# One tile of tokens summed in PSUM by a one-hot product over all experts; gate products and gate loads ahead of up; two shared groups before the expert loop and four inside it

## The reference

```python
scores = sigmoid(xt @ w_router)                       # xt = h, 544 tokens; 128 experts
_, idx = top_k(scores + b_router, 8)
gate = sel / sum(sel) * 2.5                           # sel = scores of the eight picked
h = silu(xb @ w_e1[e]) * (xb @ w_e3[e])               # xb: the tokens of expert e; 1024 -> 256
yb = (h @ w_e2[e]) * w[:, None]                       # w: their gates; 256 -> 1024
routed = zeros.at[tok].add(yb)                        # over all experts
shared = (silu(xt @ w_s1) * (xt @ w_s3)) @ w_s2       # one shared expert of 256
y = layer_norm(ALPHA * h + shared + routed)
```

## Time and profile before

| | us |
|---|---|
| median of three runs | 1943.91 |
| the profiled execution | 1941.7 |
| its span (first to last instruction) | 1939.9 |
| expert loop, first product to last output product | 825.3 to 1887.5 |
| busy: PE, DVE, ACT, POOL | 1777.5, 603.8, 392.7, 366.2 |
| mean granted TensorE clock | 0.966 |

### The profile page before, as it was taken

The page is one execution under the profiler, slowest core; times in us unless marked ns, Lnnn a source line. Parts: engine busy times, 40 slices in busy tenths (PEclk is TensorE's granted clock), DMA queues, the critical chain, the costliest instruction groups (busy, mean ns, idle before and its releaser), DMA issues.

```text
span 1939.9 us, 29734 instructions
## 1 busy us (share of the span) xinstructions
PE 1777.5 (92%) x10770; PEld 1051.4 (54%) x10770; DVE 603.8 (31%) x1504; ACT 392.7 (20%) x928; POOL 366.2 (19%) x529
## 2 busy tenths in 40 slices
PE   7999999999999999997899999988888888888887
PEld 6857778888888874643444444433333333333332
DVE  1296756873234213521122112211111111111113
ACT  0114455551221002211111111111111111111112
...
GB/s 122 141 133 120 87 66 50 3 36 53 137 80 134 87 61 207 223 335 421 421 419 413 417 413 412 419 407 400 412 397 410 409 411 404 407 399 416 399 406 238
DMA packets 162463, 529.82 MB, mean 273 GB/s; under 512 B 22173, under 2 KB 89039, under 8 KB 111821
## 3 DMA queue, kind: packets, MB, share of 16 engines
...
## 4 chain that ended last, share of the span: by engine, by line
PE 55%; DMA 36%; DVE 3%; SPq 2%; issue 2%; ACT 1%; DVEq 1%; ACTq 0%; POOLq 0%
DMA arena<-in_w_e 35%; PE bank L2088 14%; PE bank L1460 9%; PE bank L522 5%; PE bank L1467 5%; PE bank L558 4%; PE bank L1218 4%; PE bank L1951 3%; SPq L1376 2%; PE bank L547 1%; PE bank L2011 1%; PE bank L2106 1%; PE bank L1977 1%; DVEq L1326 1%; DVE arena L932 1%
## 5 line engine op out<-in xcount | busy, mean ns | idle before, releaser
L2088 PE MATMUL bank<-arena 128*64 128x512 f32 x2048 | 505.1, 651 | 122.5 <-DMA arena<-in_w_e 121.2
L2088 PEld LDWEIGHTS bank<-arena 128*64 128x64 f32 x2048 | 157.6, 149 | 459.7 <-issue 458.0
L2106 PE MATMUL bank<-arena 128*64 128x512 f32 x1024 | 233.9, 599 | 0.0
L1921 POOL DMA_INDIRECT arena<-h_rows,index x66 | 66.9, 1013 | 777.8 <-DVE index L2245 721.1
L2380 DVE TENSOR_TENSOR arena<-bank,arena 128x256 f32<-128x256 f32 x64 | 27.2, 425 | 551.6 <-ACT arena L2205 551.6
L1460 PE MATMUL bank<-arena 128*128 128x276 f32 x768 | 182.6, 396 | 0.0
L1460 PEld LDWEIGHTS bank<-arena 128*128 128x128 f32 x768 | 146.0, 190 | 32.0
L2205 ACT ACTIVATE arena<-bank 128x256 f32<-128x256 f32 x64 | 24.7, 386 | 607.2 <-PE bank L2088 607.2
L2106 PEld LDWEIGHTS bank<-arena 128*64 128x64 f32 x1024 | 67.9, 137 | 110.8 <-issue 109.6
L1218 PE MATMUL bank<-arena 64*64 64x64 f32 (+2 forms) x2816 | 116.6, 237 | 8.5 <-DVE arena L1324 3.4
L1218 PEld LDWEIGHTS bank<-arena 64*64 64x64 f32 x2816 | 103.8, 135 | 13.8 <-DVE arena L1324 4.8
...
## 6 DMA issues: line engine op xcount, KB each, us to landing
arena<-in_w_e SPq DMA_DIRECT2D x384, 1024.0 KB, 14.5
...
```

Source lines behind the costliest of these rows:

```text
L1921: pool.indirect_dma_start(xg[:, v, :], None, io["h_rows"][:, :], bass.IndirectOffsetOnAxis(ap=m.index[:, w, 0:1], axis=0), bounds_check=NT ...
L2088: mm = pe.matmul(p_gu[t * S:(t + 1) * S, :], xt[:, v, c, t * S:(t + 1) * S], w13[2 * v + t][:, :, c, :], start=(c == 0), stop=(c == KD - 1))
L2106: mm = pe.matmul(p_y[h][t * S:(t + 1) * S, :], hidT[:, j, t * S:(t + 1) * S], w2[2 * v + t][:, j, h * 512:(h + 1) * 512], start=(j == 0), ...
```

## The change

- **Tile 0 in PSUM.** For the first tile (`SUMMED = 1`) the scaled output rows of a pair are not scattered. DVE compares the token numbers of the pair's slots with 0 to 127 (`spread`, 128 x 128, one column per token), and PE multiplies that one-hot matrix with the pair's scaled output rows, accumulating over all pairs in banks 4 and 5 (`spread_rows`, two products of 128x512 per pair, one pair behind). The rank column of these tokens is 0, so their scatter index is out of bounds and the row is skipped. Shared expert and ALPHA * h of tile 0 are added in the same banks (`shared_rows`), without a copy to `res`; tile 0 has no rank loads, no `summed` and no folds.
- **Banks.** To make room, `turn` uses one bank in two halves (ACT copies the first before PE writes the second), the hidden rows are turned into the bank of the slots (so PE waits until DVE has read the slots), and the two halves of the output use one bank one after the other (so the second half waits until DVE has scaled the first).
- **Gate first.** The gate product (256 columns) comes before the up product, each with a semaphore of its own for its loads; SP issues the two gate loads of pair n + 2 after the gate product, the two up loads after the up product.
- **Order.** The slot search moves between the two half turns. Two shared groups stand ahead of the loop, four follow in pairs 6, 8, 10 and 12. The first products of the queue places no longer stand behind a shared half.

The core of the diff:

```diff
-O_LOW = ((O_HT, O_HT + PART), (O_WEXP[0], O_WEXP[0] + PART), (O_WEXP[1], O_WEXP[1] + PART),
-         (O_WEXP[0] + 2 * PART, O_WEXP[1] + 2 * PART))
-O_MID = tuple((O_WEXP[x] + y * PART, O_WEXP[x] + y * PART + D) for x in (2, 3) for y in (0, 1))
-O_HIGH = tuple((o, o + D) for o in (O_WEXP[2] + 2 * PART, O_WEXP[3] + 2 * PART, O_XG, O_XTE))
-O_SPART = O_W2S
+SUMMED = 1
+O_LOW = {1: (O_HT, O_HT + PART), 2: (O_WEXP[0], O_WEXP[1]), 3: (O_WEXP[0] + PART, O_WEXP[1] + PART)}
+O_MID = {1: (O_W2S, O_W2S + D), 2: (O_WEXP[0] + 2 * PART, O_WEXP[0] + 2 * PART + D),
+         3: (O_WEXP[1] + 2 * PART, O_WEXP[1] + 2 * PART + D)}
+O_HIGH = {1: (O_WEXP[2], O_WEXP[2] + D), 2: (O_WEXP[2] + PART, O_WEXP[2] + PART + D), 3: (O_WEXP[3], O_WEXP[3] + D)}
+BASE_DONE = 17 + 2 * (NTT - SUMMED)
+O_SPART = O_WEXP[3] + PART
...
-EARLY_GROUPS = ((0, 0, 3), (0, 1, 7), (0, 2, 6))
+EARLY_GROUPS = ((0, 0, 3), (0, 1, 2))
...
-    p_slot, p_turn, p_gu, p_ht, p_y = m.ps[0], m.ps[1:3], m.ps[3], m.ps[4], m.ps[5:7]
+    p_slot, p_turn, p_gu, p_y = m.ps[0], m.ps[1], m.ps[2], m.ps[3]
+    p_ht = p_slot[:, 8:8 + 2 * P]
...
+        return m.ps[(4, 6, 0, 2, 4)[i] + h]
...
         def load(r, done, v, e):
+            sp.wait_ge(s_gate, NP * r + done + 1)
+            for t in range(2):
+                load_w1(sp, m, io, e + t, 2 * v + t, 0, s_w1[v][0])
             sp.wait_ge(s_gu, NP * r + done + 1)
             for t in range(2):
-                load_w13(sp, m, io, e + t, 2 * v + t, s_w13[v])
-            sp.wait_ge(s_y, NP * r + done + 1)
+                load_w1(sp, m, io, e + t, 2 * v + t, 1, s_w1[v][1])
+            sp.wait_ge(s_y1, NP * r + done + 1)
             for t in range(2):
                 load_w2(sp, m, io, e + t, 2 * v + t, s_w2[v])
...
+        sp.wait_ge(s_base, BASE_DONE)
+        sp.wait_ge(s_out[1], (16 * NP // 2) * count)
+        ranks(1, O_LOW, 0, 4, s_low)
+        sp.wait_ge(s_xt, 2 * NP * count)
+        for i in (2, 3):
             ranks(i, O_LOW, 0, 4, s_low)
-
-        def high(i):
-            ranks(i, O_HIGH, 6, 2, s_high)
-
-        sp.wait_ge(s_base, 2 * NTT + 17)
-        sp.wait_ge(s_out[1], (16 * NP // 2) * count)
-        low(0)
-        sp.wait_ge(s_xt, NP * count)
-        low(1)
-        low(2)
         sp.wait_ge(s_out[0], (16 * NP // 2) * count + 16)
-        low(3)
-        sp.wait_ge(s_gu, NP * count)
-        for i in range(NTT - 1):
+        for i in (1, 2, 3):
             ranks(i, O_MID, 4, 2, s_mid)
         sp.wait_ge(s_out[1], (16 * NP // 2) * count + 16)
-        high(0)
-        high(1)
-        sp.wait_ge(s_in[1], (16 * NP // 2) * count + 16)
-        high(2)
-        sp.wait_ge(s_xt, NP * count + 1)
-        high(3)
+        for i in (1, 2, 3):
+            ranks(i, O_HIGH, 6, 2, s_high)
...
         def shared_late(i):
-            pe.wait_ge(s_sa, i + 3)
-            shared_half(0, 1, i * THIRD, O_HT - 4 * THIRD, 7)
-            shared_half(1, 1, i * THIRD, O_HT - 4 * THIRD, 7).then_inc(s_sh, 1)
+            j, x = (0, 2) if i == 0 else (1, i - 1)
+            pe.wait_ge(s_sa, 2 + i)
+            shared_half(0, j, x * THIRD, O_HT, 7)
+            shared_half(1, j, x * THIRD, O_HT, 7).then_inc(s_sh, 1)
+        def shared_rows(t, h):
+            for j in range(2):
+                pe.matmul(final_bank(t, h)[:, :], sact[:, j, t * P:(t + 1) * P], w2s[:, j, h * 512:(h + 1) * 512],
+                          start=False, stop=False)
+            for k in range(4):
+                mm = pe.matmul(final_bank(t, h)[:, k * P:(k + 1) * P], hT[:, 4 * h + k, t * P:(t + 1) * P], alpha,
+                               start=False, stop=False)
+            mm.then_inc(s_bp, 1)
...
+        def spread_rows(v, h, first=False, last=False):
+            return pe.matmul(final_bank(0, h)[:, :], spread[:, v, 0, :], yg[:, v, h * 512:(h + 1) * 512], start=first, stop=last)
...
-        def turn(v):
-            for c in range(KD):
-                mm = pe.transpose(p_turn[c // 4][:, (c % 4) * P:(c % 4 + 1) * P], xg[:, v, c::KD], m.ident[:, :])
+        def turn(v, x):
+            for c in range(4 * x, 4 * x + 4):
+                mm = pe.transpose(p_turn[:, (c % 4) * P:(c % 4 + 1) * P], xg[:, v, c::KD], m.ident[:, :])
             mm.then_inc(s_t, 1)
...
-        shared(0, 2)
-        shared(1, 2)
+        pe.wait_ge(s_yv, 1)
+        for h in range(2):
+            spread_rows(1, h, first=True)
         count = rounds(pe)
         pe.wait_ge(s_in[0], 16)
-        turn(0)
-        pe.wait_ge(s_sa, 1)
-        pe.wait_ge(sem("shared_down_loaded"), 16)
+        turn(0, 0)
+        pe.wait_ge(s_xt, 1)
+        turn(0, 1)
+        pe.wait_ge(s_sa, 2)
...
-                    pe.wait_ge(s_w13[v], (64 * NP // 2) * r + 64 * i + 64)
-                    pe.wait_ge(s_xt, NP * r + n + 1)
-                    for c in range(KD):
-                        for t in range(2):
-                            mm = pe.matmul(p_gu[t * S:(t + 1) * S, :], xt[:, v, c, t * S:(t + 1) * S],
-                                           w13[2 * v + t][:, :, c, :], start=(c == 0), stop=(c == KD - 1))
-                    mm.then_inc(s_gu, 1)
+                    pe.wait_ge(s_xt, 2 * NP * r + 2 * n + 2)
+                    for x in range(2):
+                        pe.wait_ge(s_w1[v][x], (32 * NP // 2) * r + 32 * i + 32)
+                        for c in range(KD):
+                            for t in range(2):
+                                mm = pe.matmul(p_gu[t * S:(t + 1) * S, x * DE:(x + 1) * DE], xt[:, v, c, t * S:(t + 1) * S],
+                                               w13[2 * v + t][:, x, c, :], start=(c == 0), stop=(c == KD - 1))
+                        mm.then_inc((s_gate, s_gu)[x], 1)
                     pe.wait_ge(s_in[1 - v], (16 * NP // 2) * r + 16 * i + 16 * v + 16)
-                    turn(1 - v)
+                    turn(1 - v, 0)
+                    pe.wait_ge(s_hc, NP * r + n + 1)
+                    find_slots(NP * r + n + AHEAD, n + AHEAD, v)
+                    pe.wait_ge(s_xt, 2 * NP * r + 2 * n + 3)
+                    turn(1 - v, 1)
                     pe.wait_ge(s_hid, NP * r + n + 1)
+                    pe.wait_ge(s_idx, NP * r + n + AHEAD + 2)
                     for j in range(2):
                         mm = pe.transpose(p_ht[:, j * P:(j + 1) * P], hid[:, j::2], m.ident[:, :])
                     mm.then_inc(s_ht, 1)
-                    find_slots(NP * r + n + AHEAD, n + AHEAD, v)
-                    pe.wait_ge(s_w2[v], (32 * NP // 2) * r + 32 * i + 32)
-                    pe.wait_ge(s_hc, NP * r + n + 1)
                     pe.wait_ge(s_yv, NP * r + n + 1)
                     pe.wait_ge(s_ya, NP * r + n + 1)
-                    for j in range(2):
-                        for h in range(2):
+                    spread_rows(1 - v, 0)
+                    pe.wait_ge(s_w2[v], (32 * NP // 2) * r + 32 * i + 32)
+                    pe.wait_ge(s_hc, NP * r + n + 2)
+                    for h in range(2):
+                        if h == 1:
+                            spread_rows(1 - v, 1)
+                            pe.wait_ge(s_yv, NP * r + n + 2)
+                        for j in range(2):
                             for t in range(2):
-                                mm = pe.matmul(p_y[h][t * S:(t + 1) * S, :], hidT[:, j, t * S:(t + 1) * S],
+                                mm = pe.matmul(p_y[t * S:(t + 1) * S, :], hidT[:, j, t * S:(t + 1) * S],
                                                w2[2 * v + t][:, j, h * 512:(h + 1) * 512], start=(j == 0), stop=(j == 1))
-                    mm.then_inc(s_y, 1)
+                        mm.then_inc((s_y, s_y1)[h], 1)
                     with pe.If((NP // 2) * r + i < 13):
                         if v == 0:
-                            with pe.If(i < 7):
-                                with pe.If(i > 3):
-                                    shared_late(i)
+                            for g in range(4):
+                                with pe.If(i < 4 + g):
+                                    with pe.If(i > 2 + g):
+                                        shared_late(g)
                         with pe.If(i > 7):
-                            pe.wait_ge(s_base, 2 * i + (v + 1))
+                            pe.wait_ge(sem("shared_down_loaded"), 16)
+                            pe.wait_ge(s_base, 17)
                             for t in range(NTT):
                                 with pe.If(i < 9 + t):
                                     with pe.If(i > 7 + t):
-                                        base(t, v)
-
-        pe.wait_ge(s_idx, NP * count + 3)
-        pe.wait_ge(s_xt, NP * count + 1)
-        pe.wait_ge(s_hc, NP * count)
+                                        (shared_rows if t < SUMMED else base)(t, v)
         pe.wait_ge(s_yv, NP * count + 1)
         pe.wait_ge(s_ya, NP * count + 1)
-        pe.wait_ge(s_base, 2 * NTT + 17)
-        for i in range(NTT - 1):
+        for h in range(2):
+            mm = spread_rows(1, h, last=True)
```

(43 more changed lines are left out.)

84 lines of the change are left out of this document (42 added, 42 removed).

## The result

The changed kernel takes **1929.5 us** (median of 5 runs, 1924.5 to 1933.2), the kernel before 1943.8 beside it (5 runs, 1939.5 to 1947.0): ratio **0.9926**, 95% interval 0.9911 to 0.994. It is 14.4 us faster, where 23.6 were forecast; the time lies in the range (1898 to 1942). In the two profiles the spans are therefore only 9.8 us apart.

A forecast was written before the change was run, and what follows sets the result against it. Before, the loop was taken as bound by loads (16.81 us a pair, TensorE 13.08). Gains of 2.5 (head), 12.6 (loop) and 8.5 (end) sum to 23.6, so 1943.9 becomes 1920 us, range 1898 to 1942.

The forecast's parts named there:

- TensorE's pair: TensorE's work for one pair in the expert loop: 15.5 us, bounds 14.9 to 16.5, against 13.08 before.
- work moved in: Four shared groups and ten base products, moved into pairs 6 to 25 of the loop: 48 us of TensorE.
- Head: Before the loop: one shared group goes, spread zeros and half turns come; 2.5 us gained, bounds 0 to 4.
- stall of 0.27 before the hidden turn: In TensorE's pair: new wait for VectorE's slots in the shared bank, 2.01 us against 1.74 covered.
- stall of 0.24: In TensorE's pair, before the output's second half: wait for eviction of the one output bank, beyond the spread product.
- Loads: Loop's period where loads set the pace: 16.3 us a pair, against 16.81 before.
- bounds of 16.1 and 16.65: Loop's load period: 16.1 us if all 16 DMA engines stay full, 16.65 if lagging engines keep their lag.
- the first rival: Loop: loads don't yield, period 16.65 us, time 1932; sign: an up pair's last landing ten us after its first; chance 0.19.
- End: From last output to the end: 8.5 us gained from 52.4; 24.0 us until tile 1 is whole.
- a price for rank loads that still bind: At the end: if rank loads still bind, the gain is 5 us in place of 8.5.
- Everything hides: Rival for the loop: TensorE's pair 14.9 us, period 16.1, time 1897 on the median; chance 0.14.
- TensorE bound for all 64 pairs: Rival for the loop: shared-bank turns make TensorE the bound throughout; at 16.3 us a pair, 1962; chance 0.15, 0.10 slower.

The follow-up runs named there:

- experiment 7: Changed kernel without both `spread_rows` of the loop, so its result lacks tile 0's routed experts: 1933.8 us, ratio 0.9938.
- experiment 8: Changed kernel, but SP holds the gate weights' loads until the up product is done, so all four leave together: 1934.9 us, ratio 0.9953.
- experiment 6: Changed kernel with the moved work spread and picked behind an inner loop of four pairs, and a second bank for the output: 1901.7 us, ratio 0.9786.
- experiment 9: Kernel before, with each expert's slots handed out in turn to groups of four partitions: 1920.2 us, ratio 0.9892.
- experiment 5: Changed kernel with the same moved work spread over the loop, its tests standing behind an inner loop of four pairs: 1908.7 us, ratio 0.9821.
- experiment 2: Changed kernel, but tile 0's routed rows are also scattered to memory as before, not read back: 1949.6 us, ratio 1.0023.
- experiment 10: Changed kernel with moved work spread behind an inner loop of four pairs, two output banks, and slots handed out in turn: 1896.5 us, ratio 0.9761.
- 1: Kernel before with gate-first alone: own loads, semaphore and product for the gate weights: 1943.1 us, ratio 0.9988.

## Why the prediction held, and what was mis-sized

By its own steps, in the profiled execution (us; the last output is 11.5 later than forecast, the end's own part 2.3):

| step | forecast | measured |
|---|---|---|
| loop starts | 822.8 | 824.57 |
| pair 0 to pair 1 | 15.5 | 19.13 |
| TensorE's pair | 15.5 | 15.28 |
| work moved in, pairs 6 to 25 | 48 | 52.1 |
| pairs 1 to 15 and 26, beside 15.28 each | none | 3.9 |
| pair 27 starts | 1289.3 | 1297.0 |
| period where loads bind | 16.3 | 16.22 |
| last output | 1872.4 | 1883.9 |
| from there to the end | 43.9 | 46.2 |

*Head.* TensorE was already 2.1 us later than in the profile of before at the first of the shared and output products ahead of the routing (725.8 against 723.7), before anything that the change touches. Set against that, the gain is 0.7 + 2.1 = 2.8 us where 2.5 were forecast, so this step was right.

*Pair 0, a part that the forecast didn't have.* TensorE is idle for 3.62 us with "issue", and the product behind takes 8.81 us for 7.1: the granted clock from 844 to 850 is 0.72, so part of it runs at 1.2 GHz. (In experiment 7 the gap is 3.68 and the product behind it takes 7.13, so the two don't always come together.) Around that gap the profile's instruction queue moves one packet of 16 KB, while loads fill the DMA. With all four loads released together ahead of it the gap is 5.85 (experiment 8); with the branch's code moved out of the pair the gap isn't there, and one appears where that code stands, 4.27 us behind the first four pairs and the first shared group (experiment 6):

```profile
896.94 9.51 PE L2135 MATMUL bank<-arena 128*64 128x256 f32 x64 [4.27 <-issue]
```

That it is a fetch of code behind queued loads fits all three; no run held the loads back, so it is argued, not shown.

*TensorE's pair.* 15.28 for 15.5, from the rows above. The product was forecast at 7.06, from one that had waited before (7.02). The changed kernel's first one, which had waited too, takes just that, 831.63 - 824.57 = 7.06:

```profile
824.57 7.13 PE L2115 MATMUL bank<-arena 128*64 128x256 f32 x64 [0.83 <-ACT arena L2212]
831.63 0.71 PE L2057 MATMUL bank<-ident,arena 128*128 128x128 f32 x4
```

Without a wait before it is 7.00, where 512 columns take 6.96 (859.42 - 852.46 in experiment 9). So twice as many products cost 0.04 us. By the Trainium skill's 2.5 ns a product (TensorE: Matmul & The Clock Gate, section "Wait — 56ns, not 53.3ns?") it would be 0.08, an estimate; the trace shows half of that. Search and half turn take 1.03 + 0.71 = 1.74, so the stall of 0.27 before the hidden turn isn't there. The two spreads take 0.96 + 1.05, 0.3 more than their 0.86 each, about the forecast's stall of 0.24.

*Work moved in.* The forecast's own terms give 47.5 (4 x 5.06 + 10 x 2.73), which it rounded up to 48. The shared groups take 5.19 each, 0.1 more than forecast. A base product costs 3.14 in its pair ((1281.57 - 1097.41) - 10 x 15.28 = 31.4 for ten), 0.4 more than the 2.7 taken from the earlier trace rows, since tests stand between it and the product before: one gap there is 0.85, and without tests in the pairs (experiment 5) it costs 2.98. Shared groups and base products together are 52.1. In pairs 1 to 15 and 26 another 3.9 us go: 1.9 in pair 1, most of it for the product at the lower clock (843.70 to 860.89), and 2.0 for tests where no item is due. So this part is 8 us over the forecast's 48. All of it is on the path, because TensorE sets the pace here. A shorter pair hid part of that: 27 pairs at 0.22 under the forecast gave 5.9 back, which is luck.

*Loads.* The value chosen with least ground, between bounds of 16.1 and 16.65, was nearly exact: 16.22 for 16.3. Experiments 2 and 9 fit its reason: the rows of tile 0 stood at the low partitions, which every expert fills first, and slots handed out in turn alone gave two thirds of the same gain in the period. The gate and up loads issued between 1540 and 1860 now take 19.4 to 28.9 us to land (before 6.9 to 25.4), so none comes far ahead of the others. The two up loads of one pair, issued at 1551.2 and 1551.6, land 5.8 us apart, where ten was the first rival's sign; that rival (16.65) is refuted. From pair 27 to the last up landing 571.4 was forecast and 574.8 measured. What the forecast had wrong in this step is where the waits begin: it looked for them from pair 27 on, and they come from pair 42 on. For the time that is the same, since the DMA is full from 1303 on either way; TensorE's lead only puts its waits off.

*End.* It took 46.2 us for the forecast 43.9. From the eviction to tile 1's first copy it was 24.5 us (1884.7 to 1909.2, the row below) for 24.0; then TensorE waited 2.03 us for the high ranks of tile 2. ScalarE's and TensorE's rows of the changed kernel:

```profile
1909.19 0.60 ACT L2259 ACTIVATE arena<-bank 128x512 f32<-128x512 f32 x1 [12.59 <-PE bank L2035]
```
```profile
1911.17 5.42 PE L2035 MATMUL bank<-arena 128*64 128x512 f32 x16 [2.03 <-DMA arena<-routed_rows]
```

That wait is most of the difference; where it is nearly gone, in experiment 10, the end takes 43.4. The forecast had a price for rank loads that still bind (47.4), but it looked at tile 1, where it was tile 2.

*The other rivals.* "Everything hides" failed in pairs 0 to 26 (15.28, not 14.9, and 56 us of moved work). "TensorE bound for all 64 pairs" held to pair 41 by TensorE's waits, and only to pair 27 by the loads, which are full from there.

So the forecast was right in its mechanism: TensorE, then loads, with the crossing after the moved work. The gain was 14.4 us where 23.6 were forecast, and two terms were too small: the moved work with its tests and the slow product (48 forecast, 56 measured), and the first pair (15.5 forecast, 19.1 measured). And the forecast counted 48 us of moved work as a price of TensorE without asking what it cost the DMA: 21 us lay there to be had by placing it otherwise (experiment 5). Where the gain comes from is measured: skipping the scatter is worth 20 us, the changed kernel without it is 6 slower than before (experiment 2); gate-first gives 5 at most (1 and 8), and the tile sum costs the kernel nothing that the runs can tell (7).
